# Tile 3's ranking cut into pieces inside the expert loop, and the modulation's row products on four column quarters

## The chip, the cores and the metric
The kernel runs on one core of a Trainium2 chip. The metric is the device time of one execution in microseconds; lower is better. The kernel before takes 2369.66 us (median of 3 runs, 2368.72 to 2372.24).

## The reference, cut to what matters
Two transformer layers over 512 tokens of width 1024, in float32. The first ends in a PEER layer, a mixture of 16384 small experts; the second takes its normalised input through a modulation vector.

```python
q = (h @ w_q).reshape(B, S, PEER_HEADS, 2, PEER_KEY_DIM)
sc = jnp.einsum('bshpd,phnd->bshpn', q, keys)
v1, i1 = lax.top_k(sc[..., 0, :], PEER_TOPK)
v2, i2 = lax.top_k(sc[..., 1, :], PEER_TOPK)
cand = (v1[..., :, None] + v2[..., None, :]).reshape(...)      # 16 x 16 sums per head
best, pos = lax.top_k(cand, PEER_TOPK)
idx = jnp.take_along_axis(cidx, pos, axis=-1)
gates = jax.nn.softmax(best, axis=-1)
...
act = gelu(einsum('tkd,td->tk', u[idx], h)); out = einsum('tk,tkd->td', gates * act, v[idx])

mod = jax.nn.silu(c) @ ada_w[l] + ada_b[l]                    # 1024 -> 3072
shift, scl, gate = jnp.split(mod, 3, axis=-1)
h = rms_norm_2(x, norm_g[l]) * (1.0 + scl[:, None, :]) + shift[:, None, :]
```

Each token takes 8 heads of 16 experts: 128 rows of u and 128 rows of v, of 4 KB each.

## The kernel before, in words
Everything in question stands in one block of the program, the expert stage (lines 1227 to 1712), with a queue of instructions written out by hand for each engine. Waits between the engines are counts on semaphores, and each engine works through its own queue in order.

The 512 tokens are four tiles of 128. Tiles 0 and 1 (ND = 2) are computed densely: for each of 128 panels of 128 experts, TensorE makes the hidden values (`hidden(j)`, L1632), ScalarE takes them out of a PSUM bank with a gelu (`panel(j)`, L1589; there are two banks, j % 2), VectorE multiplies them by the gates (`weigh_panel`, L1500) and TensorE multiplies by v (`outputs(j)`, L1643). Tiles 2 and 3 (NG = 2) are computed by gathers: GpSimd issues an indirect DMA for each of 256 groups of 128 rows of u and as many of v (L1375, 512 KB each), VectorE takes a dot product with each row of u (L1511) and adds each row of v, weighted (L1532). Eight slots take rows of u and eight take rows of v. Both kinds of work run in one loop, g = 0 to 129, with two gathered rows of u and two of v and one dense panel per step. Tile 2 is used from g = 0, tile 3 from g = 64.

Before that loop stand, in this order on each queue:
- **VectorE** ranks the four tiles in the order 2, 0, 1, 3 (`ORD`). `rank(x)` (L1409) adds the candidates, finds the best 16 per head by maxima, their places and replacement (`top16`, L1155 to L1175), subtracts the maximum (L1423, semaphore `shifted`) and prepares index distances (L1437). `finish(x)` (L1442) waits for the exponential (`expd`), normalises the gates and reduces the distances (L1451); for tiles 2 and 3 it also writes the row numbers for the gathers (L1458 to L1465, semaphore `expert`). The order is rank 0, rank 1, finish 0, rank 2, finish 1, rank 3, finish 2, finish 3, and then the modulation vector (L1475 to L1477), a copy of the transposed indices (L1480), and 64 steps of one-hot selectors (L1488, L1492).
- **TensorE** turns the token rows (L1622), makes the modulation: six groups of eight matmuls with one column of weights and 512 columns of data (L1681), each followed by the turn of the group before it into columns (`columns`, L1673); then nine hidden panels, the transposes of indices and gates (L1649; they wait for tiles 0 and 1 finished), and 64 steps of gate building (L1699), with 16 hidden panels among them.
- **ScalarE** copies the token rows (L1564), applies the silu to c (L1574), copies each of the six rows out (L1579), and does the exponentials (`gate_exp`, L1571) of the first three ranked tiles behind row copies 0, 3 and 5; then nine panels, with the fourth tile's exponential behind panel 7; then the copies of the gate tables (L1600).
- **SP** loads the modulation's weights, four panels of 512 KB per group, two groups ahead (L1347: group g waits for the products of group g - 2), one panel of u behind each of the last three groups (L1341), and stores the gate tables (L1356). In the loop it loads u, v and gate tables.
- **GpSimd** may issue six gathers of u and four of v early; the others wait until the gate tables are stored, for their slots share memory with these (L1384).

```python
for x in range(NT):
    rank(x)
    if x:
        finish(x - 1)
finish(NT - 1)
...
for g in range(6):                                  # ScalarE
    ...
    nc.scalar.activation(ada_row[:, g % 2], ps[0:1, 2 + g % 2], ACT.Copy).then_inc(S["ada_copied"], 1)
    if g in (0, 3, 5):
        gate_exp((0, 3, 5).index(g))
```

Of the kernel before, what the change touches and what calls it, by code (L numbers as in the profile page):

```python
# [26 lines left out]
P = 128  # L27
# [50 lines left out]
def program(nc, io):  # L78
# [1149 lines left out]
    with ExitStack() as st:  # L1228
# [47 lines left out]
        size["ada_row"] = (size["junk"][0] + 8 * D, 2 * T)  # L1276
        arena = sb(st, "arena", [P, x0 + max(w_rank, w_gates, w_late)])

        def cut(name, dt=F32):
# [34 lines left out]
        ada_row = cut("ada_row")[0:1].rearrange("p (x n) -> p x n", x=2)  # L1314
        c_act = sb(st, "c_act", [P, KD])
# [8 lines left out]
                 "c_act ada_rows ada_copied ada_columns")  # L1324
# [46 lines left out]
        @block.gpsimd  # L1371
        def _(pool):
            def fetch(dst, table, rows, n, landed):
                t, k = divmod(n, NPICK)
                nc.gpsimd.indirect_dma_start(  # L1375
                    out=dst, out_offset=None, in_=table,
                    in_offset=bass.IndirectOffsetOnAxis(ap=rows[:, t, k:k + 1], axis=0)).then_inc(landed, 16)

            def fetch_u(n):
                if n % NPICK == 0:  # L1380
                    pool.wait_ge(S["expert"], n // NPICK + 1)
                if n == U_EARLY:
# [12 lines left out]

            for n in range(U_EARLY):
                fetch_u(n)
                if n >= LAG:
                    fetch_v(n - LAG)
            for n in range(U_EARLY, NP_ + LAG):  # L1400
                if n < NP_:
                    fetch_u(n)
                fetch_v(n - LAG)

        @block.vector
        def _(v):
# [34 lines left out]

            def finish(x):  # L1442
# [10 lines left out]
                if t < ND:  # L1453
                    ins.then_inc(S["picked"], 1)
                else:
                    step(ins)
                    e, (swap_a, swap_b) = expert[:, t - ND], (u_row[:, NG + a] for a in range(2))
                    step(nc.vector.scalar_tensor_tensor(out=e, in0=ptile[:, x % 2, 1], scalar=float(EXP_N), in1=ptile[:, x % 2, 0],  # L1458
                                                        op0=ALU.mult, op1=ALU.add))

                    nc.vector.tensor_scalar(swap_a, e, 2, 0x60, ALU.logical_shift_right, ALU.bitwise_and)
                    nc.vector.tensor_scalar(swap_b, e, 2, 0x180, ALU.logical_shift_left, ALU.bitwise_and)
                    step(nc.vector.tensor_scalar(u_row[:, t - ND], e, 0x3e1f, None, ALU.bitwise_and))
                    step(nc.vector.tensor_tensor(swap_a, swap_a, swap_b, ALU.bitwise_or))
                    nc.vector.tensor_tensor(u_row[:, t - ND], u_row[:, t - ND], swap_a, ALU.bitwise_or).then_inc(S["expert"], 1)  # L1465

            for x in range(NT):
                rank(x)
                if x:
                    finish(x - 1)  # L1470
            finish(NT - 1)
# [3 lines left out]
            step(nc.vector.tensor_tensor(mod[:], ps[:, 7, 0:24], vecs[:, a:a + 24], ALU.add))  # L1475
# [8 lines left out]
            for n in range(NSTEP):  # L1484
# [8 lines left out]
                ins.then_inc(S["colhot"], 1)  # L1493

# [46 lines left out]

            weigh_panel(0)
            for g in range(EXP_N + 2):
# [15 lines left out]
        def _(act):  # L1559
# [14 lines left out]
            nc.scalar.activation(c_act[:], vecs[:, a:a + KD], ACT.Silu).then_inc(S["c_act"], 1)  # L1574
            for g in range(6):
# [3 lines left out]
                nc.scalar.activation(ada_row[:, g % 2], ps[0:1, 2 + g % 2], ACT.Copy).then_inc(S["ada_copied"], 1)  # L1579
# [25 lines left out]
            for j in range(EXP_N):  # L1605
# [13 lines left out]
        def _(pe):  # L1619
# [50 lines left out]
            def columns(g):  # L1670
                pe.wait_ge(S["ada_copied"], g + 1)
                for i in range(4):
                    mm = nc.tensor.matmul(ps[:, 7, 4 * g + i:4 * g + i + 1], ada_row[:, g % 2, i * P:(i + 1) * P], ident[0:1, 0:1],  # L1673
                                          start=True, stop=True)
                mm.then_inc(S["ada_columns"], 1)
            for g in range(6):
# [3 lines left out]
                for k in range(KD):  # L1680
                    mm = nc.tensor.matmul(ps[0:1, 2 + g % 2], c_act[:, k:k + 1], ada_w[:, g % 2, :, k], start=k == 0, stop=k == KD - 1)  # L1681
# [58 lines left out]
    with ExitStack() as st:  # L1740
# [14 lines left out]
        def two_norms(ahead):  # L1755
# [3 lines left out]
            with ExitStack() as sn:  # L1759
# [564 lines left out]
```

## Time and profile before

| | us |
|---|---|
| median of 3 runs | 2369.66 |
| span of the profiled execution | 2367.7 |
| ranking and modulation, from its first instruction to the start of gate building | 641 to 741 |
| gate building | 741 to 862 |
| expert loop | 862 to 1885 |
| the second layer | 1885 to 2368 |

The span runs from the first to the last instruction of the core in one profiled execution. What lies around it is not recorded for that execution; the median of the runs is 2.0 us above it. Busy time over the whole span: TensorE 86%, VectorE 67%, GpSimd 35%, ScalarE 20%. These are averages over stages with different limits, so the rows below are by stretch. One fp32 matmul leaves two records on TensorE. The granted clock stands as a share of 2.4 GHz: 1.00 is 2.4 GHz, 0.50 is 1.2 GHz. All times in the views are us from the span's start.

### The profile page before, as it was taken

The page shows a single profiled execution, that of the slowest core. Times are in us where ns is not written, and L with a number is a line of the kernel's source. Part 1 is how long each engine was busy: PE and PEld are TensorE (multiplying, and loading weights), DVE is VectorE, ACT ScalarE, POOL GpSimd, SP SyncE. Part 2 cuts the span into 40 slices and gives each one's busy share as a digit, 9 for nine tenths or more (in the row PEclk, how much of TensorE's full clock was granted, in tenths as well). Part 3 has the DMA queues.
Part 4 walks back from the last instruction along what each step waited for, and adds up shares of the span by engine and source line. Part 5 has one row for each costly group of instructions (what it writes and reads, how often), then busy time and mean ns, then how long its engine had stood idle before and what let it go on. Part 6 is the DMA issues. An engine that isn't in the chain of part 4 may idle for free. (4 is left out here: it accounts for less than half of the span.)

```text
span 2367.7 us, 24354 instructions
## 1 busy us (share of the span) xinstructions
PE 2040.2 (86%) x8002; PEld 1359.9 (57%) x8002; DVE 1585.8 (67%) x3456; ACT 477.7 (20%) x1073; POOL 828.9 (35%) x633
## 2 busy tenths in 40 slices
PE   5998779959798989989998889888866579999987
PEld 4875568748537966555655555555522257734455
DVE  4568745568999966666666666666777875346664
ACT  3344122122212320000000000000000132334551
POOL 3420034433110025665555455544566422300002
PEclk8997589979899989999999999999988789989998
DMA  7986879667473669999999999999999622100002
GB/s 285 356 307 214 274 287 390 232 256 260 167 292 122 217 262 396 402 402 402 402 402 403 404 402 402 402 403 404 402 401 401 253 95 85 54 36 1 1 1 71
DMA packets 203900, 648.09 MB, mean 274 GB/s; under 512 B 19840, under 2 KB 52736, under 8 KB 202496
## 3 DMA queue, kind: packets, MB, share of 16 engines
q1 hardware_dynamic: 118384, 335.60, 37.9%
q0 software_dynamic: 73728, 268.47, 28.8%
q10 hardware_dynamic: 11664, 42.47, 5.2%
q8 instruction: 65, 1.06, 0.2%
q14 instruction: 59, 0.48, 0.1%
HBM read 560.48 MB, written 85.98 MB: 273 GB/s over the span
## 5 line engine op out<-in xcount | busy, mean ns | idle before, releaser
L1643 PE MATMUL ps<-arena 128*128 128x512 f32 x1024 | 509.9, 645 | 150.3 <-DVE arena L1500 101.0
L1511 DVE CUSTOM_DVE_ANT_0 arena<-arena 128x1024 bf16<-128x1024 f32 x256 | 313.3, 1225 | 247.7 <-DMA arena<-u_rows,u_row 132.4
L1632 PE MATMUL ps<-rows_n,arena 128*128 128x256 f32 x2048 | 464.7, 379 | 0.0
L1632 PEld LDWEIGHTS ps<-rows_n,arena 128*128 128x128 f32 x2048 | 386.9, 190 | 95.7 <-issue 49.7
L1643 PEld LDWEIGHTS ps<-arena 128*128 128x128 f32 x1024 | 204.4, 206 | 400.9 <-issue 263.5
L1375 POOL DMA_INDIRECT arena<-u_rows,u_row x256 | 284.8, 1113 | 313.1 <-DMA gates<-arena 168.4
L1375 POOL DMA_INDIRECT arena<-in_v,expert x192 | 207.1, 1078 | 324.3 <-DVE arena L1532 297.2
L1532 DVE SCALAR_TENSOR_TENSOR arena<-arena,wt 128x1024 f32<-128x1024 f32 x192 | 246.2, 1283 | 0.5
L192 DVE STREAM_TRANSPOSE tdst<-tsrc 128x1024 f32<-128x1024 f32 x128 | 155.4, 1230 | 85.5 <-DMA u_rows<-tdst 41.0
L1609 ACT ACTIVATE ge<-dots 128x2 f32<-128x2 f32 x128 | 26.0, 203 | 909.7 <-DVE dots L1511 909.7
L237 POOL TENSOR_TENSOR in_wlo<-in_raw,in_whi 128x1024 fp32r<-128x1024 f32 x45 | 114.1, 2538 | 234.5 <-ACT in_whi L233 234.5
L237 POOL TENSOR_TENSOR mg_wlo<-mg_raw,mg_whi 128x1024 fp32r<-128x1024 f32 x32 | 79.6, 2490 | 255.1 <-ACT mg_whi L233 255.1
L488 PE MATMUL ps<-act_hi,in_whi 128*128 128x512 f32 x360 | 99.6, 421 | 32.0 <-PEq L258 16.0
L1500 DVE TENSOR_TENSOR arena<-arena 128x256 f32<-128x256 f32 x128 | 53.6, 420 | 100.7 <-DMA arena<-gates 100.6
L237 POOL TENSOR_TENSOR o_wlo<-o_raw,o_whi 128x1024 fp32r<-128x1024 f32 x8 | 21.1, 2643 | 238.8 <-ACT o_whi L233 238.8
L488 PEld LDWEIGHTS ps<-act_hi,in_whi 128*128 128x128 f32 x360 | 70.1, 199 | 51.3 <-issue 35.6
L488 PE MATMUL ps<-act_lo,in_whi 128*128 128x512 f32 x360 | 93.7, 403 | 0.0
L488 PE MATMUL ps<-act_hi,in_wlo 128*128 128x512 f32 x360 | 90.2, 392 | 0.0
L233 ACT ACTIVATE in_whi<-in_raw 128x1024 fp32r<-128x1024 f32 x45 | 47.4, 1058 | 179.8 <-PE ps L488 179.8
L1375 POOL DMA_INDIRECT rows_n<-in_v,expert x64 | 65.3, 1020 | 50.6 <-DVE arena L1532 41.0
L488 PEld LDWEIGHTS ps<-act_lo,in_whi 128*128 128x128 f32 x360 | 70.9, 197 | 16.8
L1532 DVE SCALAR_TENSOR_TENSOR arena<-rows_n,wt,arena 128x1024 f32<-128x1024 f32 x62 | 79.5, 1282 | 0.0
(409 smaller groups left out, 2936.4 us busy)
## 6 DMA issues: line engine op xcount, KB each, us to landing
tsrc<-in_u SPq DMA_DIRECT2D x128, 512.0 KB, 7.8
u_rows<-tdst SPq DMA_DIRECT2D x128, 512.0 KB, 6.2
arena<-in_u SPq DMA_DIRECT2D x128, 512.0 KB, 10.7
arena<-in_v SPq DMA_DIRECT2D x128, 512.0 KB, 12.1
in_raw<-in_panels ACTq DMA_DIRECT2D x37, 512.0 KB, 4.2
gates<-arena SPq DMA_DIRECT2D x8, 2048.0 KB, 8.8
arena<-gates SPq DMA_DIRECT2D x32, 512.0 KB, 18.7
mg_raw<-in_panels ACTq DMA_DIRECT2D x28, 512.0 KB, 6.8
```

The lines of the kernel that those rows point to most:

```text
L192: nc.vector.transpose(tdst[:, x % NDST].rearrange("p (x l) -> p x l", l=32), blocks[:, :, b]).then_inc(self.turned, 1)
L233: nc.scalar.activation(self.hi[:, i % 2], self.raw[:, i % RING], ACT.Copy).then_inc(self.hi_ready, 1)
L237: nc.gpsimd.tensor_tensor(self.lo[:, i % 2], self.raw[:, i % RING], self.hi[:, i % 2].bitcast(F32), ALU.subtract).then_inc(self.lo_ready, 1)
L488: mm = nc.tensor.matmul(bank, w[:, i % 2, k - ks[0] + s.get("w0", 0)], a[:, k], start=x == 0 and k == ks[0], stop=x == 2 and k == ks[-1])
L1375: nc.gpsimd.indirect_dma_start(out=dst, out_offset=None, in_=table, in_offset=bass.IndirectOffsetOnAxis(ap=rows[:, t, k:k + 1], axis=0)).t ...
L1500: nc.vector.tensor_tensor(w, w, gj[:, b % 2, :, j % GB], ALU.mult).then_inc(S["w"], 1)
L1511: nc.vector.tensor_tensor_reduce(out=junk[:, n % 2], in0=u_slot[n % NU], in1=hrows[:, n // NPICK], scale=1.0, scalar=0.0, op0=ALU.mult, op ...
L1532: nc.vector.scalar_tensor_tensor(out=out, in0=row, scalar=by, in1=out, op0=ALU.mult, op1=ALU.add).then_inc(S["pv"], 1)
L1609: nc.scalar.activation(ge[:, j % 2], dots[:, j % 2], ACT.Gelu).then_inc(S["gelu"], 1)
L1632: mm = nc.tensor.matmul(ps[:, j % 2, 0:TD], ud[:, j % RJ, k], rows_n2[:, 0, k], start=k == 0, stop=k == KD - 1)
L1643: mm = nc.tensor.matmul(ps[:, 4 + 2 * t + c], park[:, j % NPK, t * P:(t + 1) * P], vd[:, j % RJ, c * T:(c + 1) * T], start=j == 0, stop=j ...
```

## The change
Four things are changed, all in or behind the expert stage.

1. The ranking and finishing of the last ranked tile (tile 3) leaves its place ahead of gate building. It becomes a generator, `rank_last`, cut into 23 pieces, and the loop calls `next` on it once per step from g = 2. The distances are made in eight pieces of two heads instead of two of eight heads. Its buffers lie in the memory of the bf16 constants `cb`, which the loop doesn't use, and in tile 3's accumulator. Its exponential moves on ScalarE from behind panel 7 to behind step 20 of the loop (`LATE_EXP`).
2. The modulation's row products: the weights become 32 columns wide, of which the first holds silu(c) and the others are zero (GpSimd clears them, and the silu waits for that). Of the eight matmuls of a group, number k writes partitions 32 (k % 4) to 32 (k % 4) + 31 of the bank, so that two matmuls add up in each quarter.
3. The four partial rows are copied out together (128 rows instead of one), and `columns` adds them with a column of 1/128 as data; VectorE multiplies by 128 when it adds the bias.
4. The constants `cb` are loaded again, behind the four first weight loads of the second layer's norm, and SP waits for them.

```diff
+        size["c_act"] = (size["junk"][0] + 8 * D + 2 * T, KD * 32)
...
-        ada_row = cut("ada_row")[0:1].rearrange("p (x n) -> p x n", x=2)
-        c_act = sb(st, "c_act", [P, KD])
+        ada_row = cut("ada_row").rearrange("p (x n) -> p x n", x=2)
+        LATE_EXP = 20
+        spare = cb[:].bitcast(F32)
+        l_cand = spare[:, 0:HEADS * NCAND].rearrange("p (h c) -> p h c", h=HEADS)
...
+        l_rest = acc[:, NG - 1, 0:HEADS * NCAND].rearrange("p (h c) -> p h c", h=HEADS)
+        l_far = acc[:, NG - 1, 0:512].rearrange("p (h k j) -> p h k j", h=2, k=TOPK)
+        c_act = cut("c_act").rearrange("p (k m) -> p k m", k=KD)
...
+            nc.gpsimd.memset(cut("c_act"), 0.0).then_inc(S["c_zero"], 1)
...
-            for x in range(NT):
+            for x in range(NT - 1):
                 rank(x)
                 if x:
                     finish(x - 1)
-            finish(NT - 1)
+            finish(NT - 2)
...
-            step(nc.vector.tensor_tensor(mod[:], ps[:, 7, 0:24], vecs[:, a:a + 24], ALU.add))
+            step(nc.vector.scalar_tensor_tensor(out=mod[:], in0=ps[:, 7, 0:24], scalar=float(P), in1=vecs[:, a:a + 24],
+                                                op0=ALU.mult, op1=ALU.add))
...
+            def rank_last():
+                t = NT - 1
...
+                src = l_cand
+                for half in range(2):
+                    s = slice(8 * half, 8 * half + 8)
+                    for h in range(HEADS):
+                        ins = nc.vector.max(l_best[:, h, s], src[:, h])
+                    step(ins)
+                    yield
+                    for h0 in (0, 4):
+                        for h in range(h0, h0 + 4):
+                            ins = nc.vector.max_index(l_pos[:, h, s], l_best[:, h, s], src[:, h])
+                        yield
...
+                for a in range(2):
+                    for h in range(0, HEADS, 2):
+                        shape = [P, 2, TOPK, TOPK]
+                        step(nc.vector.tensor_tensor(l_far, l_idf[:, h:h + 2, a].unsqueeze(2).broadcast_to(shape),
...
+                        ins = nc.vector.tensor_reduce(l_tile[:, a, h * TOPK:(h + 2) * TOPK], l_far.rearrange("p h k j -> p (h k) j"), AX.X, ALU.min,
+                                                      apply_absolute_value=True)
+                        step(ins)
+                        yield
+                v.wait_ge(S["expd"], NT)
...
+                expert_rows(t, l_tile)
...
+            last = rank_last()
             weigh_panel(0)
             for g in range(EXP_N + 2):
...
                 if 1 <= g <= EXP_N:
                     weigh(g - 1)
+                if g >= 2:
+                    next(last, None)
...
-            nc.scalar.activation(c_act[:], vecs[:, a:a + KD], ACT.Silu).then_inc(S["c_act"], 1)
+            act.wait_ge(S["c_zero"], 1)
+            nc.scalar.activation(c_act[:, :, 0], vecs[:, a:a + KD], ACT.Silu).then_inc(S["c_act"], 1)
...
-                nc.scalar.activation(ada_row[:, g % 2], ps[0:1, 2 + g % 2], ACT.Copy).then_inc(S["ada_copied"], 1)
+                nc.scalar.activation(ada_row[:, g % 2], ps[:, 2 + g % 2], ACT.Copy).then_inc(S["ada_copied"], 1)
...
             for j in range(NPK_A):
                 panel(j)
-                if j == 7:
-                    gate_exp(3)
...
+                if j == LATE_EXP:
+                    gate_exp(NT - 1)
                 if j + NPK < EXP_N:
                     panel(j + NPK)
...
-                    mm = nc.tensor.matmul(ps[:, 7, 4 * g + i:4 * g + i + 1], ada_row[:, g % 2, i * P:(i + 1) * P], ident[0:1, 0:1],
+                    mm = nc.tensor.matmul(ps[:, 7, 4 * g + i:4 * g + i + 1], ada_row[:, g % 2, i * P:(i + 1) * P], cst("mean128")[:, 0:1],
                                           start=True, stop=True)
...
                 for k in range(KD):
-                    mm = nc.tensor.matmul(ps[0:1, 2 + g % 2], c_act[:, k:k + 1], ada_w[:, g % 2, :, k], start=k == 0, stop=k == KD - 1)
+                    q = slice(32 * (k % 4), 32 * (k % 4) + 32)
+                    mm = nc.tensor.matmul(ps[q, 2 + g % 2], c_act[:, k], ada_w[:, g % 2, :, k], start=k < 4, stop=k >= 4)
...
                     for i in range(RING):
                         ahead.load(sp, i)
+                    load_second(sp)
+                    sp.wait_ge(cb_loaded, 16)
```

## Rows read from the trace of the kernel before
**Rows 1.** Windows: stretch, length, busy us by engine, TensorE clock, DMA share, GB/s.
```profile
641.00:700.40 59.40, 53.20 (x160) 16.75 (x160) 57.10 (x253) 10.70 (x16) 9.80 (x10) 0.91 0.81 306
...
741.00:862.00 121.00, 117.82 (x768) 108.94 (x768) 107.27 (x320) 42.72 (x80) 0.00 (x0) 0.98 0.51 185
...
900.00:1100.00 200.00, 184.64 (x622) 119.08 (x621) 137.50 (x213) 14.05 (x52) 126.54 (x104) 0.97 1.03 401
```

**Rows 2.** DMA view of the expert loop, 861 to 1853 us.
```profile
DMA packets 137459, 397.92 MB, mean 401 GB/s; under 512 B 12076, under 2 KB 44844, under 8 KB 137302
```

**Rows 3.** Timeline of VectorE: start, length in us, line, operation.
```profile
696.27 0.29 DVE L1423 TENSOR_TENSOR gate<-arena 128x128 f32<-128x128 f32 x1
...
709.06 0.28 DVE L1412 CAST arena<-idx 128x256 f32<-128x256 uint32 x1
...
727.53 0.29 DVE L1445 TENSOR_REDUCE gsum<-gate 128x8 f32<-128x128 f32 x1
...
732.69 0.27 DVE L1445 TENSOR_REDUCE gsum<-gate 128x8 f32<-128x128 f32 x1
...
739.13 0.29 DVE L1465 TENSOR_TENSOR u_row<-u_row 128x128 uint32<-128x128 uint32 x1
...
739.84 0.41 DVE L1480 COPY i1T<-ps 128x256 f32<-128x256 f32 x1
```

**Rows 4.** Timeline of TensorE, 691 to 743 us.
```profile
691.58 7.03 PE L1681 MATMUL ps<-arena,c_act 128*1 128x512 f32 x16 [0.56 <-DMA arena<-in_panels]
...
698.54 1.61 PE L1673 MATMUL ps<-cf,arena 1*128 1x1 f32 x13
...
711.74 20.02 PE L1632 MATMUL ps<-rows_n,arena 128*128 128x256 f32 x92
...
732.83 0.66 PE L1649 MATMUL ps<-cf,arena 128*128 128x128 f32 x4 [1.07 <-DVE arena L1451]
...
733.32 0.38 PE L1649 MATMUL ps<-cf,gate 128*128 128x128 f32 x2
...
742.82 3.75 PE L1699 MATMUL ps<-arena 128*128 128x128 f32 x16 [9.12 <-DVE arena L1492]
```

**Rows 5.** Timeline of ScalarE, 643 to 732 us.
```profile
643.56 3.70 ACT L1564 ACTIVATE arena<-ps 128x512 f32<-128x512 f32 x4 [14.49 <-PE ps L1622]
...
699.14 0.29 ACT L1571 ACTIVATE gate<-gate 128x128 f32<-128x128 f32 x1
...
700.56 1.28 ACT L1589 ACT_TABLE_LOAD   x1 [1.13 <-PE ps L1673]
...
724.89 0.38 ACT L1589 ACTIVATE arena<-ps 128x256 f32<-128x256 f32 x1 [3.07 <-PE ps L1632]
```

**Rows 6.** TensorE and its weight loads: timeline rows, then one line's group.
```profile
297.39 0.66 PE L1016 MATMUL ps<-state,hq 128*32 128x128 f32 x8
...
246.70 0.20 PEld L1016 LDWEIGHTS ps<-state,hq 128*32 128x32 f32 x6 [0.22 <-issue]
...
L1016 PE MATMUL ps<-state,hq 128*32 128x128 f32 x8 | 0.7, 422 | 0.0
```

**Rows 7.** Windows: columns of rows 1; the first is line 1016 alone, TensorE and weight loads.
```profile
297.00:300.00 3.00, 1.31 (x16) 0.41 (x16) 0.50 1.03 404
...
643.00:650.00 7.00, 1.95 (x12) 1.74 (x11) 6.90 (x47) 5.19 (x6) 0.00 (x0) 0.74 0.97 376
...
742.80:746.40 3.60, 3.58 (x17) 3.60 (x18) 3.00 (x10) 0.60 (x1) 0.00 (x0) 0.50 0.00 0
```

**Rows 8.** VectorE in the expert loop: timeline rows, then the dots of 900 to 1100.
```profile
900.34 0.43 DVE L1500 TENSOR_TENSOR arena<-arena 128x256 f32<-128x256 f32 x1 [18.38 <-DMA arena<-gates]
...
905.40 0.07 DVE L1511 DVE_READ_ACCUMULATOR2_ANT dots<- 128x1 f32 x1
...
910.54 0.08 DVE L1511 DVE_READ_ACCUMULATOR2_ANT dots<- 128x1 f32 x1
...
L1511 DVE CUSTOM_DVE_ANT_0 arena<-arena 128x1024 bf16<-128x1024 f32 x53 | 64.6, 1219 | 8.0 <-DMA arena<-u_rows,u_row 4.2 <-issue 3.8
```

More of the change, by code:

```diff
@@ L1323, in program @@
                  "hturn hrows dot gelu weight pv h dgelu w out osum oturn oadd "
-                 "c_act ada_rows ada_copied ada_columns")
+                 "c_zero c_act ada_rows ada_copied ada_columns")
         S = dict(zip(names.split(), sems(st, " ".join("gx_" + x for x in names.split()))))
@@ L1440, in rank, with expert_rows @@
                 step(ins)
+            def expert_rows(t, tile):
+                e, (swap_a, swap_b) = expert[:, t - ND], (u_row[:, NG + a] for a in range(2))
+                step(nc.vector.scalar_tensor_tensor(out=e, in0=tile[:, 1], scalar=float(EXP_N), in1=tile[:, 0],
+                                                    op0=ALU.mult, op1=ALU.add))
+                nc.vector.tensor_scalar(swap_a, e, 2, 0x60, ALU.logical_shift_right, ALU.bitwise_and)
+                nc.vector.tensor_scalar(swap_b, e, 2, 0x180, ALU.logical_shift_left, ALU.bitwise_and)
+                step(nc.vector.tensor_scalar(u_row[:, t - ND], e, 0x3e1f, None, ALU.bitwise_and))
+                step(nc.vector.tensor_tensor(swap_a, swap_a, swap_b, ALU.bitwise_or))
+                nc.vector.tensor_tensor(u_row[:, t - ND], u_row[:, t - ND], swap_a, ALU.bitwise_or).then_inc(S["expert"], 1)
             def finish(x):
@@ L1456, in finish @@
                     step(ins)
[L1457 to L1465, printed above, removed]
-            for x in range(NT):
+                    expert_rows(t, ptile[:, x % 2])
+            for x in range(NT - 1):
                 rank(x)
@@ L1493, in _ @@
                 ins.then_inc(S["colhot"], 1)
+            def rank_last():
+                t = NT - 1
+                step(nc.vector.tensor_copy(l_idf, idx[:, t]))
+                nc.vector.scalar_tensor_tensor(out=l_idf.rearrange("p h a k -> p (h a) k"),
+                                               in0=cst("iota16").unsqueeze(1).broadcast_to([P, 2 * HEADS, TOPK]), scalar=STRIDE,
+                                               in1=l_idf.rearrange("p h a k -> p (h a) k"), op0=ALU.mult, op1=ALU.add)
+                yield
+                for a0, a1, nb, at in ((0, 4, TOPK, 0), (4, TOPK, 4, 4 * TOPK)):
+                    shape = [P, HEADS, a1 - a0, nb]
+                    ins = nc.vector.tensor_tensor(l_cand[:, :, at:at + (a1 - a0) * nb].rearrange("p h (a b) -> p h a b", b=nb),
+                                                  val[:, t, :, 0, a0:a1].unsqueeze(3).broadcast_to(shape),
+                                                  val[:, t, :, 1, 0:nb].unsqueeze(2).broadcast_to(shape), ALU.add)
+                step(ins)
[10 more added lines that the diff above has]
+                            ins = nc.vector.max_index(l_pos[:, h, s], l_best[:, h, s], src[:, h])
+                        yield
+                    if half == 0:
+                        for h0 in (0, 4):
+                            for h in range(h0, h0 + 4):
+                                ins = nc.vector.match_replace(l_rest[:, h], l_best[:, h, s], src[:, h], -3.0e38)
+                            yield
+                        src = l_rest
+                    step(ins)
+                nc.vector.tensor_tensor(gate[:, t], l_best, l_best[:, :, 0:1].broadcast_to([P, HEADS, TOPK]),
+                                        ALU.subtract).then_inc(S["shifted"], 1)
+                nc.vector.tensor_scalar(l_posh[:, 0], l_pos, 4, None, ALU.logical_shift_right)
+                nc.vector.tensor_copy(l_posx[:, 2], l_pos.rearrange("p h k -> p (h k)"))
+                step(nc.vector.tensor_scalar(l_posh[:, 1], l_pos, 2, None, ALU.logical_shift_right))
+                yield
+                step(nc.vector.tensor_copy(l_posx[:, 0:2], l_posh.rearrange("p a h k -> p a (h k)")))
+                step(nc.vector.tensor_scalar(l_posx[:, 1], l_posx[:, 1], 12.0, None, ALU.subtract))
+                step(nc.vector.tensor_tensor(l_posf[:, 0], l_posx[:, 0], l_posx[:, 1], ALU.max))
+                yield
+                step(nc.vector.tensor_scalar(l_posx[:, 3], l_posf[:, 0], 4.0, 48.0, ALU.mult, ALU.add))
+                step(nc.vector.scalar_tensor_tensor(out=l_posx[:, 3], in0=l_posf[:, 0], scalar=16.0, in1=l_posx[:, 3],
+                                                    op0=ALU.mult, op1=ALU.min))
+                step(nc.vector.tensor_tensor(l_posf[:, 1], l_posx[:, 2], l_posx[:, 3], ALU.subtract))
+                step(nc.vector.tensor_scalar(l_posf, l_posf, STRIDE, None, ALU.mult))
+                yield
+                for a in range(2):
+                    for h in range(0, HEADS, 2):
+                        shape = [P, 2, TOPK, TOPK]
+                        step(nc.vector.tensor_tensor(l_far, l_idf[:, h:h + 2, a].unsqueeze(2).broadcast_to(shape),
+                                                     l_posf[:, a].rearrange("p (h k) -> p h k", h=HEADS)[:, h:h + 2].unsqueeze(3).broadcast_to(shape),
+                                                     ALU.subtract))
+                        ins = nc.vector.tensor_reduce(l_tile[:, a, h * TOPK:(h + 2) * TOPK], l_far.rearrange("p h k j -> p (h k) j"), AX.X, ALU.min,
+                                                      apply_absolute_value=True)
+                        step(ins)
+                        yield
+                v.wait_ge(S["expd"], NT)
+                step(nc.vector.tensor_reduce(gsum[:, t], gate[:, t], AX.X, ALU.add))
+                step(nc.vector.reciprocal(gsum[:, t], gsum[:, t]))
+                nc.vector.tensor_tensor(gate[:, t], gate[:, t], gsum[:, t].unsqueeze(2).broadcast_to([P, HEADS, TOPK]),
+                                        ALU.mult).then_inc(S["gates"], 1)
+                yield
+                expert_rows(t, l_tile)
```

8 lines of the change are left out of this document (added).

## The prediction, made before the change was run
> **What bounds the kernel now.** I read the stages first. The bytes per second of the table of windows [rows 1] tell three regimes in the part that the change touches. From 900 us on the expert loop moves 401 GB/s with the DMA engines full, and the DMA view of 861 to 1853 us shows 398 MB at a mean of 401 GB/s [rows 2]: 992 us, set by bytes. The stage before it, 741 to 862 us, is TensorE's (117.8 us busy of 121) at half that traffic. Its gathers stand still, because their slots share memory with the gate tables, so a byte of the loop cannot be fetched earlier unless this stage starts and ends earlier. Then I read, engine by engine, what lets the gate stage begin at 741. VectorE ranks without a gap: tile 3's ranking is issued at 709.06, its end at 727.53, then the finish of the third ranked tile (to 732.69), the finish of tile 3 (to 739.4), and only at 739.84 the copy of the turned indices [rows 3]. TensorE had those transposes done at 733.70 (733.32 plus 0.38) and stood idle until 742.82 [rows 4]. So VectorE sets the start, by 739.84 - 733.70 = 6.1 us; right behind it is TensorE's own chain: row products to 698.6, the last columns to 700.2, nine hidden panels to 731.8, transposes to 733.7.
>
> **The change, part by part.**
> *Ranking taken out of the front.* Tile 3's rank and finish leave VectorE's queue: 18.5 us (709.06 to 727.53) and 6.7 us (732.69 to 739.42), 25.2 us [rows 3]. The finish of the third ranked tile now follows at 709.1 and lasts 5.2 us, so VectorE is ready at 714.2, the three small modulation operations 0.4 us later. From then on it is TensorE that is late: the gain is not 25 us but what TensorE's chain allows. If nothing else changed, its transposes end at 733.7 less the 1.1 us for which it waited on VectorE (731.76 to 732.83), 732.7, and the copy moves from 739.84 to 732.8: 7.0 us.
>
> *Row products on four column quarters.* Now one group of eight matmuls shows 16 records in 7.03 us, 0.44 us each, one behind the other [rows 4]. The nearest rows are the four 32-column products of line 1016: eight records in 0.66 us, 0.42 us of which is the length of one, so all eight start within 0.24 us [rows 6], at the 1.2 GHz level [rows 7]. Sixteen full-width records with the same 128 columns took 3.75 us from 742.82 at that level [rows 4, 7], eight of them 1.9 us. Quarters do run beside each other, two waves for the two fp32 records. Applied to 512 columns: a group takes 2 x 2 x 0.44 = 1.8 us at 2.4 GHz, 3.5 at 1.2. The bounds are 7.03 us (nothing gained) and 1.8; I take the lower end for the warm array, since that row is the same operation in the same type.
> The Trainium skill has a rule against this, in "TensorE: Matmul & The Clock Gate", section "Part 3: Packing small matmuls": weights load beside a running matmul only where the row groups differ, and column quarters share theirs. By it the products would stay serial and the sum would be the 7.0 us above. The trace differs: the six weight loads of one such set of three lie within 0.20 us from 246.70 [rows 6], and its matmuls, which follow their loads within a few hundredths, have all started before the first has ended.
> With 1.8 to 3.5 us of work per group the transfers become the bound: 24 panel loads of 512 KB (six groups of four; L1347) are 12.6 MB, two of the three interleaved u loads another 1.05 MB, at the 376 GB/s that the first stretch shows [rows 7] to the 401 of the loop 34 to 36 us after the first byte at 643. The last group lands at about 678, is multiplied by 681, copied in 0.6 us and turned into columns in 1.05: columns done near 683, not 700.2. The columns now load 128 rows instead of one, at the same 128 columns and count; bounds 0 and the whole 1.0 us again, I take 0.
>
> *What is late next.* ScalarE computes the exponential of the third ranked tile between its last row copy and its first panel. That exponential waits for VectorE's shift, which starts at 696.27 [rows 3] and is not made earlier by this change. Today the wait is hidden, for ScalarE is there only at 699.14 [rows 5]. Tomorrow it is there at 682 and stands until 696.6; behind it wait all panel evacuations, and TensorE can run only two hidden panels (two banks), to about 691 us. Then: exponential 0.3, table load 1.28, evacuation 0.38, so panel 2 starts at 698.6. Seven panels at 3.45 us, the 3.07 us of waiting and 0.38 of evacuation that repeat for each [rows 5], give 722.8. TensorE will have been idle for over 7 us; after the idle 9.12 us before 742.82 it ran at 0.50 for 3.6 us [rows 4, 7], so half of that is lost again: 724.6. Transposes took 0.9 us [rows 4]: 725.5, the copy at 725.7. Against 739.84 that is 14.1 us. Bounds: 7.0 if the quarters are serial; 24 if ScalarE's wait were absent (683 + 31.1 + 0.9 = 715, the copy just behind it, at 716).
>
> *Clock at the gate stage.* Its first 3.6 us ran at 0.50 [rows 7] after TensorE had idled 9.1 us. That idle time shrinks to some 3 us (the copies and the first selector tiles, 739.84 to 742.82, stay). Gain between 0 and 1.8 us; I take 0.9.
>
> *The ranking put into the loop.* 23 pieces, one per iteration from g = 2 to 24, between 915 and 1100 us. The far distances are made in eight halves of 512 elements, so some 16 more fixed costs of about 0.1 us: 27 us in all, 1.2 a piece, the heaviest (eight maxima, or the last with six small operations) about 1.6. A full iteration of VectorE takes 5.14 us (905.40 to 910.54), one in the byte-bound loop 7.5 to 8.1 (53 dots in 200 us, two an iteration, for the first) [rows 8]. 5.14 + 1.6 = 6.7 fits. The cover is the 31% of VectorE that is idle between 900 and 1100 [rows 1]. It is thin in one place: after the 18.4 us wait for the gate table, to 900.34 [rows 8], VectorE works off a backlog at full load, and gathers there wait for slots that it frees. Eight pieces at 1.2 us lie there; if all of it starved the queue, 9 us would be lost, but the stretch holds 401 GB/s with that wait in it [rows 1]; bounds 0 and 9, I take 1. ScalarE's late exponential brings two table loads (2.6 us) in one iteration of an engine that is 7% busy (14.05 of 200 us) [rows 1]: 0.
> The memory clear on POOL has until ScalarE is through with its first four copies, at 647.3 [rows 5]; POOL's only work between 641 and 700 is ten gathers [rows 1]: 0. The second load of the bf16 constants (0.85 MB, 2 us) goes behind four weight loads on SP's queue, and nothing in that norm reads them; the new wait on SP has nothing queued behind it in that block: 0.
>
> **Sum**: 14.1 + 0.9 - 1 = 14.0 us. The profiled execution's span is 2367.7 us; it becomes 2353.7. The median of the runs shown, 2369.66, is 2.0 us above that span, so I forecast 2355.6.
>
> **The rivals.**
> *Serial quarters*: each weight load waits until the quarter before it has streamed, and a group stays at 7 us. TensorE's columns are done at 700.2 as now: 7.0 - 1 + 0.5 (clock) = 6.5 us, 2363. For it: fp32 at 512 columns on quarters is nowhere in the trace. Against: [rows 6]. Chance 0.10. This is the way in which the rule of the Trainium skill quoted above would come true.
> *ScalarE doesn't hold TensorE*, or quarters and clock do better than reckoned: up to 24 us, 2346. Against it: ScalarE takes its work in program order; chance 0.06.
> *The pieces starve the loop*, which ends slower: if VectorE decided the pace between g = 2 and 24, all 27 us would come back on top, 2355.6 + 26 = 2382. It decides once an iteration of VectorE, waits included, exceeds the loop's 7.5 us, that is if a piece costs over 2.4 us; since the dots and row sums take turns waiting for landings, some of the 31% may not be usable. Half such a loss gives 2369, no change. For it: gathers of v already wait on VectorE. Against: eight slots for each of two streams, four iterations deep. Chance 0.07 for the full loss, 0.07 for about half.
> The forecast's own case has 0.70, with a range of its own of 2350 to 2360.
>
> **How the numbers follow.** About 0.2% (5 us) is what a measurement of this kernel can tell from no change. Faster by more than that: forecast 0.70, the better case 0.06, the serial one 0.10 (it lies 6.5 below): 0.86. Within: 0.07. Slower: 0.07. The range 2346 to 2364 takes in the better and the serial case and leaves out the starved ones.
>
> **What would show it.** Right: the matmuls of line 1681 as 16 records within about 2 to 4 us a group; the last columns near 683; a gap of some 7 us on TensorE before the third hidden panel, ended by ScalarE; VectorE's copy of the turned indices near 726 with its wait ended by TensorE; the loop's bytes per second at 401 with pieces in it; the end of the loop's traffic near 1839 instead of 1853. Wrong: row products still 7 us a group, a dip of GB/s or new waits of POOL on VectorE between 900 and 1100 us, or an iteration longer than 8.1 us there.

## The result, and the profile after

The changed kernel takes 2354.11 us (median of 4 runs, 2350.46 to 2355.47) against 2369.19 us of the kernel before, measured beside it: a ratio of 0.9941 with a 95% interval of 0.9924 to 0.9959, 15.1 us or 0.6% faster. The forecast was 2355.6, in a range of 2346 to 2364.

The profiled execution has a span of 2348.6 us. Single runs of one kernel differ by 5 us and more, and most of that arises before the expert stage. Its first instruction on TensorE, the turn of the token rows, comes at 641.58 us in the profile of before, at 639.11 in this one, and at 644.98 in a second profile of the same changed kernel: 5.9 of the 7.8 us by which the two spans of the changed kernel differ (2348.6 and 2356.4). So I measure stages from that instruction.

TensorE in the profile after, from the fourth of the six groups of row products to the first step of gate building (timeline: start, length, line, operation, tiles, count, idle time before; it answers to [rows 4]):

```profile
664.66 1.92 PE L1772 MATMUL ps<-arena 128*32 128x512 f32 x16 [1.30 <-DMA arena<-in_panels]
666.51 1.05 PE L1763 MATMUL ps<-cf,arena 128*128 128x1 f32 x8
671.43 3.64 PE L1772 MATMUL ps<-arena 128*32 128x512 f32 x16 [3.87 <-DMA arena<-in_panels]
675.00 1.87 PE L1763 MATMUL ps<-cf,arena 128*128 128x1 f32 x8
677.83 3.64 PE L1772 MATMUL ps<-arena 128*32 128x512 f32 x16 [0.96 <-DMA arena<-in_panels]
681.40 3.57 PE L1763 MATMUL ps<-cf,arena 128*128 128x1 f32 x16
684.83 9.72 PE L1722 MATMUL ps<-rows_n,arena 128*128 128x256 f32 x32
696.42 24.41 PE L1722 MATMUL ps<-rows_n,arena 128*128 128x256 f32 x112 [1.87 <-ACT arena L1679]
720.67 0.60 PE L1739 MATMUL ps<-cf,arena 128*128 128x128 f32 x4
721.11 0.38 PE L1739 MATMUL ps<-cf,gate 128*128 128x128 f32 x2
724.52 3.49 PE L1790 MATMUL ps<-arena 128*128 128x128 f32 x16 [3.02 <-DVE arena L1511]
```

A group of row products (L1772) is now 16 records in 1.9 us at the full clock and 3.6 at half, where one took 7.03 [rows 4], and in front of each stands a wait for a landing: the transfers set the pace. The last columns are done at 685.0. Then come two hidden panels (32 records, 9.72 us; their mean granted clock is 0.73, and at 1.00 they take 7.15 in the second profile, shown further down), a wait of 1.87 us for ScalarE, seven panels in 24.41 us, the transposes and the first gate step at 724.52.

ScalarE in the same stretch (it answers to [rows 5]):

```profile
681.53 0.60 ACT L1669 ACTIVATE arena<-ps 128x512 f32<-128x512 f32 x1 [5.80 <-PE ps L1772]
694.28 0.31 ACT L1660 ACTIVATE gate<-gate 128x128 f32<-128x128 f32 x1 [12.14 <-DVE gate L1438]
694.60 1.28 ACT L1679 ACT_TABLE_LOAD   x1
695.90 0.66 ACT L1679 ACTIVATE arena<-ps 128x256 f32<-128x256 f32 x2
```

This is the wait that the prediction named: ScalarE has copied its last row at 682.1, stands 12.14 us for VectorE's shift of the third ranked tile, and the first panel's evacuation comes only at 695.90.

VectorE (it answers to [rows 3]; L1471 is the third finish, L1496 the last modulation operation, L1499 the copy of the turned indices):

```profile
701.43 0.29 DVE L1471 TENSOR_REDUCE gsum<-gate 128x8 f32<-128x128 f32 x1
...
712.14 0.17 DVE L1496 TENSOR_TENSOR gain<-gain,vecs 128x8 f32<-128x8 f32 x1
721.53 0.42 DVE L1499 COPY i1T<-ps 128x256 f32<-128x256 f32 x1 [9.22 <-PE ps L1739]
```

VectorE is through at 712.3, idles 9.22 us and is released by TensorE. Before, the copy stood at 739.84, without a wait.

Windows of the gate stage and of the loop's first part (they answer to [rows 1]), and the DMA view of the loop (to [rows 2]):

```profile
727.00:850.00 123.00, 114.88 (x758) 105.92 (x757) 103.57 (x310) 42.34 (x80) 1.87 (x2) 0.99 0.54 196
...
900.00:1100.00 200.00, 181.94 (x613) 117.95 (x612) 152.15 (x292) 15.81 (x54) 120.49 (x102) 0.97 1.03 402
```

```profile
DMA packets 137896, 399.51 MB, mean 401 GB/s; under 512 B 12125, under 2 KB 44893, under 8 KB 137738
```

VectorE is 152.2 us busy of 200, where it was 137.5, and the rate of the transfers is unchanged at 402 GB/s. The pieces take 29 us in all, where the prediction had 27, and lie between 862.8 and 1048.3 us, so some of them ahead of this stretch. The gathers' waits for VectorE, a sign that the prediction named, did not grow: 48.4 us between 900 and 1100, against 59.0 before.

Measured from stage marks, in us (the first gate step, the last store of a gate table, the first weight load of the second layer):

| kernel | first instruction of the stage to first gate step | to last store | last store to second layer | whole |
|---|---|---|---|---|
| before | 101.2 | 203.5 | 1040.3 | 1243.8 |
| after | 85.4 | 187.2 | 1040.1 | 1227.3 |
| after, second profile | 88.5 | 189.5 | 1039.8 | 1229.3 |

(The stores are marked by the record that holds the last two of them.) The gain arises in the front, 15.8 us in one profile and 12.8 in the other, passes through gate building with 0.5 to 1.2 us on top, and through the loop untouched. The second layer lasts 482.2 us from its first load to the end, against 482.3: the second load of the constants costs nothing.

### The profile page after: what moved, and what is told of

The parts are those of the page before. It is cut to its first block and busy times, and to the rows that moved or that the text cites. A ratio compares the mean times of both kernels' runs of the same rounds, so it can differ in the third digit from the quotient of the medians.

```text
span 2348.6 us, 24367 instructions
## 1 busy us (share of the span) xinstructions
PE 2019.7 (86%) x8002; PEld 1358.1 (58%) x8002; DVE 1585.9 (68%) x3468; ACT 476.4 (20%) x1073; POOL 826.6 (35%) x634
## 5 line engine op out<-in xcount | busy, mean ns | idle before, releaser
L1390 POOL DMA_INDIRECT arena<-u_rows,u_row x256 | 279.5, 1092 | 273.9 <-DMA gates<-arena 152.0
L1586 DVE TENSOR_TENSOR arena<-arena 128x256 f32<-128x256 f32 x128 | 53.8, 421 | 86.5 <-DMA arena<-gates 85.6
```

The lines of the kernel that those rows point to most:

```text
L1390: nc.gpsimd.indirect_dma_start(out=dst, out_offset=None, in_=table, in_offset=bass.IndirectOffsetOnAxis(ap=rows[:, t, k:k + 1], axis=0)).t ...
L1586: nc.vector.tensor_tensor(w, w, gj[:, b % 2, :, j % GB], ALU.mult).then_inc(S["w"], 1)
```

## The experiments

Theory: two chains end close together in the front, VectorE's ranking and, 6 to 7 us behind it, TensorE's row products and panels; the move shortens the first, the quarters the second, and what is left is ScalarE's exponential and the half clock. Rivals: one part does it all; the pieces cost something; the quarters don't run beside each other.

**Each part alone.** `rank_only` keeps the ranking in the loop and restores the one-column products, and with them the copy of one row and the columns from it:

```diff
-                    mm = nc.tensor.matmul(ps[q, 2 + g % 2], c_act[:, k], ada_w[:, g % 2, :, k], start=k < 4, stop=k >= 4)
+                    mm = nc.tensor.matmul(ps[0:1, 2 + g % 2], c_act[:, k, 0:1], ada_w[:, g % 2, :, k], start=k == 0, stop=k == KD - 1)
```

> Only the move of tile 3's ranking into the loop; the row products stay on one column, one behind the other. Theory (two chains, VectorE first and TensorE 6 to 7 us behind it): the copy of the turned indices moves by 7.0 us against the kernel before, its wait ended by TensorE, nine hidden panels still end about 91 us after the stage's first instruction; time 2362 to 2363. Rival (the ranking alone brings it all, the quarters nothing): 14 to 15 us faster, 2354 to 2355. Rival (the pieces cost in the loop what they leave in the front): 2369.

Measured: 2361.97 us beside 2367.33, ratio 0.9973 (0.9961 to 0.9986). By the ratio that is 6.4 us; the two medians lie 5.4 apart. A group of products takes 7.03 us again. TensorE and VectorE of this kernel:

```profile
639.49 3.65 PE L1712 MATMUL ps<-cf,rows_n 128*128 128x128 f32 x16 [11.34 <-PEq L1216]
...
689.25 7.03 PE L1771 MATMUL ps<-arena 128*1 128x512 f32 x16
...
698.08 31.35 PE L1722 MATMUL ps<-rows_n,arena 128*128 128x256 f32 x144
...
733.11 1.40 PE L1789 MATMUL ps<-arena 128*128 128x128 f32 x8 [3.03 <-DVE arena L1511]
```

```profile
730.12 0.42 DVE L1499 COPY i1T<-ps 128x256 f32<-128x256 f32 x1 [17.26 <-PE ps L1739]
```

The front is 93.6 us (733.11 - 639.49), 7.6 shorter than before, and the whole 1235.7, 8.1 shorter. TensorE's panels end at 729.4, 90 us after the stage's start, and VectorE waits 17.26 us for them. The theory holds; neither rival does.

`quarters_only` does the opposite: `range(NT)` in the ranking loop, `finish(NT - 1)`, the exponential behind panel 7, no piece in the loop.

> Only the row products on column quarters; tile 3 is ranked in the front as before, and the constants are loaded again. Theory: TensorE is ahead, VectorE still reaches the copy of the turned indices 98 us after the stage's first instruction, so the time stays at 2369 within 1 us, except that TensorE may idle longer before the gate stage (0 to 2 us slower through the clock). Rival (TensorE's chain sets the front): 6 us or more faster.

Measured: 2366.51 us beside 2367.33, ratio 0.9995 (0.9982 to 1.0008). TensorE:

```profile
705.55 17.53 PE L1720 MATMUL ps<-rows_n,arena 128*128 128x256 f32 x80 [0.28 <-DMA arena<-in_u]
732.22 1.11 PE L1737 MATMUL ps<-cf,arena 128*128 128x128 f32 x4 [9.14 <-DVE arena L1477]
...
742.22 3.11 PE L1788 MATMUL ps<-arena 128*128 128x128 f32 x13 [8.46 <-DVE arena L1511]
```

Nine panels are done at 723.1, which is 82 us after the stage's start instead of 90, and then TensorE stands 9.14 us for VectorE's reduction and 8.46 us more for its selectors. The copy of the turned indices comes 98.4 us after the stage's first instruction, the front is 101.4 us and the whole 1245.0, so the theory holds. The quarters alone are worth nothing; on top of the move they are worth 7.7 us (2361.97 - 2354.30, the control beside it), and 8.4 or 6.4 by the marks (1235.7 less the 1227.3 and 1229.3 of the two profiles).

`after_again` was the control.

> The changed kernel once more, as the control for the three beside it: 2354, 15 us below the kernel before.

Measured: 2354.30 us, ratio 0.9940 (0.9918 to 0.9962).

**Is it the quarters?** `one_quarter` keeps the 32 columns of weights but sends all eight products to the same quarter (the copy takes 32 rows):

```diff
-                    q = slice(32 * (k % 4), 32 * (k % 4) + 32)
-                    mm = nc.tensor.matmul(ps[q, 2 + g % 2], c_act[:, k], ada_w[:, g % 2, :, k], start=k < 4, stop=k >= 4)
+                    q = slice(32 * (k % 1), 32 * (k % 1) + 32)
+                    mm = nc.tensor.matmul(ps[q, 2 + g % 2], c_act[:, k], ada_w[:, g % 2, :, k], start=k < 1, stop=k >= KD - 1)
```

> The changed kernel, but all eight row products of a group go to the first quarter of the array, with the same weights of 32 columns. Theory (products in different quarters run beside each other, and nothing else made them fast): a group takes 7.0 us again and the time is that of the ranking move alone, 2362. Rival (the narrow weights or the missing one-row writes made it fast, not the quarters): a group stays at 1.9 to 3.6 us and the time at 2354.

Measured: 2357.74 us, ratio 0.9957 (0.9939 to 0.9974); the whole from the marks 1235.6, as `rank_only`'s 1235.7. The median is 4 us below the expected 2362, and its interval ends at 2361 (0.9974 x 2367.18); it overlaps that of `rank_only` (0.9961 to 0.9986) and that of the changed kernel (0.9918 to 0.9962) alike, so the time decides nothing here. The marks agree with `rank_only` to 0.1 us and lie 6 to 8 us above the changed kernel's, so I go by them. Its last group on TensorE, and then the weight loads of the group at 664.66 in the profile after:

```profile
688.40 7.05 PE L1772 MATMUL ps<-arena 128*32 128x512 f32 x16
```

```profile
664.66 0.16 PEld L1772 LDWEIGHTS ps<-arena 128*32 128x32 f32 x8 [1.38 <-DMA arena<-in_panels]
665.11 0.13 PEld L1772 LDWEIGHTS ps<-arena 128*32 128x32 f32 x4 [0.30 <-issue]
665.54 0.13 PEld L1772 LDWEIGHTS ps<-arena 128*32 128x32 f32 x4 [0.30 <-issue]
```

The same instructions take 7.05 us in one quarter and 1.92 in four, 3.7 times less, both at a granted clock of 1.00. Eight weight loads go through within 0.16 us, the next eight in two sets, one with each wave of matmuls, 0.43 us apart. The Trainium skill ("TensorE: Matmul & The Clock Gate", section "Part 3: Packing small matmuls") says that a weight load runs beside a matmul in flight only where the row groups differ. Here all loads use all rows and differ in the column group alone, and the runs disagree with it: loads of one column quarter pass while the others stream.

`two_quarters` uses two.

> The changed kernel with the row products on two quarters instead of four. Theory (quarters run beside each other, and the transfers, 5 to 6 us a group, set the pace): a group takes 3.6 us at 2.4 GHz and 7.1 at 1.2, columns are done within 1 us of the four-quarter kernel if the array runs at 2.4 GHz (it is busy more of the time), and the first gate step comes 85 to 89 us after the stage's first instruction, as with four. Rival (four quarters are needed): 92 to 94 us, as with one.

Measured, in a single run: 2354.99 us, front 85.9 us (730.86 - 644.96). TensorE, two of its groups:

```profile
673.81 3.63 PE L1772 MATMUL ps<-arena 128*32 128x512 f32 x16
...
680.29 5.32 PE L1772 MATMUL ps<-arena 128*32 128x512 f32 x16 [1.87 <-DMA arena<-in_panels]
...
693.16 1.94 PE L1763 MATMUL ps<-cf,arena 64*128 64x1 f32 x16
695.04 14.35 PE L1722 MATMUL ps<-rows_n,arena 128*128 128x256 f32 x64
709.65 17.54 PE L1722 MATMUL ps<-rows_n,arena 128*128 128x256 f32 x80 [0.27 <-DMA arena<-in_u]
```

A group takes 3.63 us at the full clock, and 5.3 where the mean granted clock is 0.67. The front is that of four quarters, as expected, but not because the columns are as early. They are done 50.1 us into the stage (695.10 - 644.96), 4 to 6 us later than with four quarters; the expected 1 us had the full clock as its condition, which most groups did not get. It costs nothing because the third hidden panel can't start earlier than ScalarE lets it: TensorE's wait for it, 1.87 and 5.74 us with four quarters, is gone here, and the panels run on. So two quarters are as good as four in this kernel because of ScalarE's exponential, and with that out of the way (below) they need not be; this was not run.

**The loop's cover.** `pieces_x2` and `pieces_x4` repeat the maxima, places, replacements and distances of each piece two and four times:

```diff
+                    for rep in range(4):
+                        if rep:
+                            step(ins)
...
                     for h in range(HEADS):
                         ins = nc.vector.max(l_best[:, h, s], src[:, h])
```

> The changed kernel with the maxima, places, replacements and distances of every piece done twice, 23 us more VectorE work between the third and the twenty-fourth step of the loop. Theory (pieces hide while a step of VectorE stays under 7.5 us; 5.1 + 2 x 1.2 is 7.5): 0 to 3 us slower than the changed kernel, 2354 to 2357. Rival (pieces already cost what they take, hidden by chance elsewhere): 23 us slower, 2377.

> The same with every piece done four times, 70 us more. Theory (threshold at 2.4 us a piece): steps of 9 to 11 us against 7.5, so 20 to 38 us slower than the changed kernel, and the DMA rate falls below 400 GB/s between 900 and 1100 us. Rival (the gathers' slots hold so much that VectorE can make up for it later): under 10 us slower, DMA rate unchanged.

Measured: 2353.69 us, ratio 0.9940 (0.9924 to 0.9957), and 2378.18 us, ratio 1.0047 (1.0032 to 1.0062). From last store to second layer 1040.2 us with two, 1066.9 with four, against 1040.1. Windows of both (stretch, length, busy of TensorE, weight loads, VectorE, ScalarE, POOL, clock, DMA share, GB/s), first with two:

```profile
900.00:920.00 20.00, 19.89 (x70) 12.86 (x69) 19.86 (x70) 1.43 (x6) 11.87 (x12) 1.00 1.04 399
920.00:940.00 20.00, 19.90 (x68) 12.44 (x67) 19.93 (x63) 1.43 (x6) 12.62 (x12) 1.00 1.03 402
940.00:960.00 20.00, 18.83 (x62) 11.28 (x61) 19.86 (x62) 0.95 (x4) 11.48 (x10) 1.00 1.03 405
```

```profile
920.00:940.00 20.00, 16.00 (x48) 9.53 (x48) 19.76 (x89) 0.95 (x4) 8.97 (x8) 0.91 0.95 346
...
1020.00:1040.00 20.00, 14.41 (x37) 8.04 (x38) 19.55 (x30) 0.95 (x4) 8.97 (x8) 0.83 0.79 292
```

With the work doubled VectorE is full from 900 to 960 us (19.9 of 20 us) and the transfers don't notice. With four times the work the DMA engines fall to 292 GB/s and the loop takes 26.8 us more. The times are as both theories have them. The repeated operations stand in 16 of the 23 pieces and take 21.9, 43.9 and 87.5 us in the three kernels, so 22 and 66 us were added, a little less than the expected 23 and 70.

The length of a step, from one product with the gates (L1586, L1596 in these two) to the next, shows the threshold. In the changed kernel it is 5.9 to 6.7 us with a piece in it, and a wait for a gate table in every fourth step brings the mean to 7.9, the pace of the transfers. Doubled, eight steps in a row with distances take 8.0 us each and cost nothing; with four times the work the steps take 9.4 to 11.3 us. A step without a piece and without a wait takes 5.1 us [rows 8], so a piece may cost 2.9 us and may not cost 4.3. The pieces as they are, up to 1.6 us, are well on the safe side.

**What holds the front now.** `exp_behind_panel2` moves the third ranked tile's exponential on ScalarE:

```diff
-                if g in (0, 3, 5):
-                    gate_exp((0, 3, 5).index(g))
+                if g in (0, 3):
+                    gate_exp((0, 3).index(g))
...
             for j in range(NPK_A):
                 panel(j)
+                if j == 2:
+                    gate_exp(2)
```

> The changed kernel with the third ranked tile's exponential moved on ScalarE from ahead of panel 0 to behind panel 2. Theory: the 1.9 us for which TensorE stood before its third hidden panel go, the copy comes 1.9 us earlier relative to the stage's start, and the time is 2 us lower, 2352; the rest of the loss that was put down to this wait is in the clock of the first two panels and stays. Rival (ScalarE's wait costs the full 7 us that the prediction gave it): 5 to 7 us lower, 2348.

Measured: 2350.37 us, ratio 0.9936 (0.9913 to 0.9958), which by itself doesn't tell it from the control. The marks do: front 82.1 us, 3.3 less than one profile of the changed kernel and 6.3 less than the other; whole 1225.4, 1.9 and 3.9 less, as gate building and the loop together take 1.3 and 2.4 us more than in those profiles. ScalarE:

```profile
693.55 0.38 ACT L1679 ACTIVATE arena<-ps 128x256 f32<-128x256 f32 x1 [3.07 <-PE ps L1724]
693.96 1.28 ACT L1660 ACT_TABLE_LOAD   x1
695.25 0.31 ACT L1660 ACTIVATE gate<-gate 128x128 f32<-128x128 f32 x1
695.58 1.28 ACT L1679 ACT_TABLE_LOAD   x1
698.00 0.38 ACT L1679 ACTIVATE arena<-ps 128x256 f32<-128x256 f32 x1 [1.13 <-PE ps L1724]
```

The exponential with its two table loads fits between two evacuations. The whole agrees with the theory's 2 us against the first profile; the time, 3.9 us below the control with overlapping intervals, decides neither for it nor for the rival. One part of the theory failed: the loss in the clock of the first panels did not stay, for here the first three ran at 1.00 (48 records in 10.61 us). TensorE then stood twice for a load of u, 0.7 and 0.8 us, and no longer for ScalarE. To see why the front gains 3.3 us against one profile and 6.3 against the other, here are the two stretches of panels in the second profile of the changed kernel, with their clock, and then the same stretches' clock in the first profile:

```profile
689.40 7.15 PE L1722 MATMUL ps<-rows_n,arena 128*128 128x256 f32 x32
702.28 27.47 PE L1722 MATMUL ps<-rows_n,arena 128*128 128x256 f32 x112 [5.74 <-ACT arena L1679]
```

```profile
689.40:696.60 7.20, 7.15 (x34) 5.98 (x33) 7.09 (x46) 0.00 (x0) 5.67 (x6) 1.00 0.67 216
702.30:706.50 4.20, 4.20 (x10) 3.39 (x11) 4.13 (x4) 0.12 (x1) 0.00 (x0) 0.50 1.02 414
```

```profile
684.80:694.60 9.80, 9.76 (x33) 7.83 (x33) 9.66 (x68) 0.31 (x1) 7.51 (x8) 0.73 0.87 291
...
696.40:721.50 25.10, 25.07 (x118) 21.91 (x118) 15.60 (x17) 2.85 (x8) 0.00 (x0) 1.00 0.65 234
```

In the second profile the first two panels ran at 2.4 GHz (7.15 us), TensorE then stood 5.74 us, and the seven panels began at 1.2 GHz and took 27.47. In the first, the two ran partly at 1.2 GHz, which filled the wait (9.72 us and 1.87 of standing), and the seven stayed at 2.4 GHz (24.41). In both the seven panels begin 57.3 us into the stage, when ScalarE lets them, so the slower first two cost nothing and the whole 3 us of difference lie in the seven. `products_twice` was to settle this: each group of products is done twice.

> The changed kernel with every group of row products done twice (the second overwrites the first), to keep the array busy between the landings. Theory (two profiles of the changed kernel differ by 3 us in the front because the clock falls either before the first two hidden panels or after them): first two panels at 7.1 us, then some 5 us of standing behind ScalarE, then seven panels in 27.5 us because the clock falls then; first gate step at 88 to 89 us from the stage's first instruction. Rival (the clock does not decide it): 85 us.

Measured, in a single run: 2355.34 us, front 85.4 us. TensorE's panels:

```profile
693.35 7.15 PE L1722 MATMUL ps<-rows_n,arena 128*128 128x256 f32 x32
701.33 24.41 PE L1722 MATMUL ps<-rows_n,arena 128*128 128x256 f32 x112 [0.83 <-ACT arena L1679]
```

The expectation of 88 to 89 us failed, and the reason is in these rows: the doubled products delayed the panels, so TensorE stood only 0.83 us behind ScalarE, and the clock didn't fall. The number is the rival's, but the seven panels begin 57.3 us into the stage, as in the other two, and take 24.41 us where no long wait comes before. In three profiles the clock fell after a wait of 5.74 us and not after 1.87 or 0.83; that the wait is the cause is not shown, as no run set its length by itself.

**A version that is faster still.** `exp2_npk7` is `exp_behind_panel2` with seven instead of nine panels ahead of gate building (`NPK_A = 7`, the memory laid out as it was):

> The changed kernel with the third tile's exponential behind panel 2 and seven hidden panels ahead of gate building instead of nine; two panels move into the loop. Theory: TensorE reaches the transposes some 5 to 6 us earlier, where VectorE's finish becomes the bound again; the loop has 1.05 MB more to fetch at 401 GB/s, 2.6 us; in all 2 to 3 us below the kernel with the exponential moved, 2348 to 2350. Rival (TensorE has no room in the loop for 6.9 us more): no gain or a loss of up to 2 us.

Measured: 2345.92 us, ratio 0.9917 (0.9900 to 0.9934). Once more:

> The kernel with the exponential moved and seven panels ahead, once more, to narrow its interval: 21 us below the kernel before, 2346, ratio 0.991.

Measured: 2348.05 us, ratio 0.9913 (0.9899 to 0.9926). TensorE in the first of the two:

```profile
637.78 3.65 PE L1714 MATMUL ps<-cf,rows_n 128*128 128x128 f32 x16 [11.33 <-PEq L1216]
...
710.68 0.66 PE L1741 MATMUL ps<-cf,arena 128*128 128x128 f32 x4 [0.65 <-DVE arena L1477]
711.18 0.38 PE L1741 MATMUL ps<-cf,gate 128*128 128x128 f32 x2
714.59 3.68 PE L1792 MATMUL ps<-arena 128*128 128x128 f32 x16 [3.03 <-DVE arena L1511]
```

The front is 76.8 us (76.6 in the second profile), the stretch from last store to second layer 1043.5, and the whole 1222.4. Two panels less take 5.3 us off the front (82.1 to 76.8) and put 2.9 us into the loop (1040.6 with nine), against 2.6 expected. The transposes now wait 0.65 us for VectorE, so its chain is the bound of the front again, as the theory says. The kernel is 20 us faster than the one before. Against the changed kernel it is some 6 us faster by the medians; the intervals overlap at their ends, but the whole from the marks says the same, 1222.4 and 1222.7 against 1227.3 and 1229.3. Against `exp_behind_panel2` only the marks tell it, 1225.4.

## Why the prediction was right

- **Two chains, the move alone worth 7.0 us.** Measured 7.6 in the front; by the times it is 6.4 (ratio) or 5.4 (medians). The step from "25.2 us leave VectorE" to "7.0 us are gained" is right.
- **Quarters at 1.8 us a group, 3.5 at half clock.** Measured 1.9 and 3.6. The neighbouring rows of 32-column products [rows 6] priced it; the serial rival, given 0.10, did not come.
- **Transfers become the bound, columns done 41 us into the stage** (683 less 641.6). The bound is right, the size was short: 45.9 and 44.5 us. Groups two to six waited 1.0 to 3.9 us each for a landing in the first profile. The last group began 38.7 us into the stage in both profiles, where the prediction had 36.4 (678 less 641.6); the bytes moved up to then hold three panels of u, where it counted two. The rest is mostly the clock: the last group took 3.64 us where 3 were taken, and the last two groups of columns together 3.57 and 2.30, against 1.94 at full clock in the kernel before. It cost nothing in the end, as ScalarE's wait was longer.
- **What is late next: ScalarE's exponential.** Right in place and in releaser, and in time: the third panel was to start 57.0 us into the stage (698.6 - 641.6) and started at 57.3 in both profiles. TensorE was to stand over 7 us; it stood 1.87 and 5.74, as it was later itself. The 1.8 us booked for a half clock behind the wait were nothing in one profile and 3.1 us in the other (27.47 less 24.41). The prediction lies between the two, and that is in part luck. The copy was to come 84.1 us into the stage (725.7 - 641.6); it came at 82.4 and 85.5.
- **Clock at the gate stage, 0.9 us.** 0.5 and 1.2 by the marks.
- **Pieces in the loop, 1 us taken, 0 to 9 allowed.** Measured 0 within 0.5, and 0 for twice the work. The rival that starves the loop needs a piece of over 2.4 us by the prediction. Four times the work showed the mechanism, at 26.8 us. The threshold was placed a little low: pieces of 2.9 us cost nothing yet, and the pace of the transfers is 7.9 us a step, not 7.5. The pieces were also expected between 915 and 1100 us, but began at 862.8, the first ahead of the long wait for the gate table; nothing came of it.
- **Sum: 14.0 us.** Measured 15.1. The marks give 16.5 and 14.5 in two profiles. The terms did not all come out one by one: late columns were hidden, the half clock came in one profile only, and the loss of 1 us in the loop did not come.

Not tried: making VectorE's shift of the third tile itself earlier, and loading the modulation's weights before the expert stage, whose memory they share.

## What to carry to other kernels

Work taken off the engine that ends last gains only the distance to the engine that ends next, so follow each queue of the stage to its end before counting; a second change that is worth nothing alone (the quarters) can double the first. Work can move for free into a stage bound by transfers as long as one step of the engine that takes it stays below the step of the transfers, and doubling the moved work is a cheap way to measure the margin. After a move, look at which small operation stands, in program order, between two engines that now meet earlier.

## What the runs showed of the hardware

Four fp32 matmuls in different column quarters, with 128 rows and 512 columns each, run almost fully beside each other, weight loads included: 1.92 us for eight, where a quarter of the 7.05 us in one quarter is 1.76, and 3.63 in two.

The granted clock fell to 1.2 GHz in some groups of row products between landings and not in others of the same kernel; the dense work that followed began at either level, here 7.15 or 9.72 us for the same two panels. Where the clock falls behind a wait, the front of one kernel was 3 us longer than where it falls ahead of it.

With eight slots for each of the two streams of gathers, the DMA engines stayed at 399 to 405 GB/s while VectorE, which frees the slots, was completely full for 60 us.
